# A tuned transformer kernel: the norm's root mean square applied to a product's output, and weight loads issued one stage earlier

## The reference

```python
def rmsnorm(x, g):
    y = x * lax.rsqrt(jnp.mean(x * x, axis=-1, keepdims=True) + EPS)
    return y * g

def swiglu(h, w_in, w_out):                       # w_in 1024 x 5632, w_out 2816 x 1024
    gate, up = jnp.split(h @ w_in, 2, axis=-1)
    return (jax.nn.silu(gate) * up) @ w_out

for i in range(2):                                # first block
    x = x + 0.5 * swiglu(rmsnorm(x, ffn_norm[i, 0]), ffn_w_in[i, 0], ffn_w_out[i, 0])
    h = rmsnorm(x, mix_norm[i])
    x = x + (chunked_sgu, pool_mixer)[i](h, ...)  # both begin with h @ w_in
    x = x + 0.5 * swiglu(rmsnorm(x, ffn_norm[i, 1]), ffn_w_in[i, 1], ffn_w_out[i, 1])
x = rmsnorm(x, final_norm)
```

## Time and profile before

| | us |
|---|---|
| median of 3 runs (3184.03 to 3192.28) | 3188.72 |
| the profiled execution | 3189.99 |
| its span | 3188.0 |
| PE busy in the span | 2776.1 (87%) |
| DVE busy | 1315.2 (41%) |
| ACT busy | 887.9 (28%) |
| mean granted clock of PE | 0.934 |

### The profile page before, as it was taken

One profiled execution on the slowest core, in us unless ns is written; L12 is line 12 of the kernel. 1 busy time (PEld: TensorE's weight loads), 2 busy tenths in 40 slices (PEclk: granted clock), 3 DMA queues, 4 the chain that ended last, 5 costly groups with the idle time before them and its releaser, 6 DMA issues. The chain is left out here.

```text
span 3188.0 us, 44602 instructions
## 1 busy us (share of the span) xinstructions
PE 2776.1 (87%) x18276; PEld 2130.9 (67%) x18276; DVE 1315.2 (41%) x1781; ACT 887.9 (28%) x960; POOL 8.6 (0%) x13
## 2 busy tenths in 40 slices
PE   7989889899889967566999999999999699776888
PEld 6989889899779936354444444444444388666887
DVE  4534445455355412543324322222122338134893
ACT  4424334254234311231111112122112162122441
POOL 0000000000000000000000000000000000000000
PEclk9999899999989978686999999999999899988999
DMA  5635346345245571107999999999999533320551
GB/s 178 234 109 159 119 145 236 109 159 183 95 155 184 218 271 80 53 1 276 417 415 416 416 415 416 416 417 418 417 417 418 209 106 119 133 105 13 173 197 66
DMA packets 278879, 724.10 MB, mean 227 GB/s; under 512 B 18913, under 2 KB 177197, under 8 KB 243789
## 3 DMA queue, kind: packets, MB, share of 16 engines
q1 hardware_dynamic: 278434, 722.34, 59.7%
q10 hardware_dynamic: 330, 0.10, 0.0%
HBM read 721.35 MB, written 1.05 MB: 227 GB/s over the span
## 5 line engine op out<-in xcount | busy, mean ns | idle before, releaser
L505 PE MATMUL bank<-h_high,weight_parts 128*128 128x256 f32 x4352 | 785.3, 283 | 7.4 <-DVE weight_parts L493 7.4
L505 PEld LDWEIGHTS bank<-h_high,weight_parts 128*128 128x128 f32 x4352 | 672.9, 189 | 9.3 <-issue 9.0
L493 DVE TENSOR_TENSOR weight_parts<-weight_slots,weight_parts 128x2048 fp32r<-128x2048 f32 x208 | 472.7, 2289 | 342.6 <-ACT weight_parts L487 342.6
L487 ACT ACTIVATE weight_parts<-weight_slots 128x2048 fp32r<-128x2048 f32 x208 | 394.7, 1911 | 546.3 <-DMA weight_slots<-in_ffn_w_in 192.4
L2119 PE MATMUL bank<-weight_slots,item_x 128*64 128x512 f32 x2176 | 476.1, 595 | 0.7 <-ACT item_x L2192 0.7
L505 PE MATMUL bank<-h_part,weight_parts 128*128 128x256 f32 x1680 | 476.1, 283 | 0.0
L2119 PEld LDWEIGHTS bank<-weight_slots,item_x 128*64 128x64 f32 x2176 | 153.7, 137 | 298.8 <-issue 298.0
L2275 DVE TENSOR_TENSOR expert_sum_then_keys<-bank,expert_sum_then_keys 128x512 f32<-128x512 f32 x136 | 84.5, 684 | 625.8 <-PE bank L2158 625.8
L505 PE MATMUL bank<-hidden_high,weight_parts 128*128 (+1 forms) x1760 | 314.0, 280 | 3.8 <-DVE weight_parts L493 3.8
L505 PEld LDWEIGHTS bank<-h_part,weight_parts 128*128 128x128 f32 x1680 | 317.1, 189 | 0.1
L505 PEld LDWEIGHTS bank<-hidden_high,weight_parts 128*128 128x128 f32 x1760 | 270.8, 189 | 4.2 <-issue 4.2
(11 more groups left out here) (446 smaller groups left out, 2707.3 us busy)
## 6 DMA issues: line engine op xcount, KB each, us to landing
weight_slots<-in_w_mlp SPq DMA_DIRECT2D x408, 1024.0 KB, 21.1
weight_slots<-in_ffn_w_in SPq DMA_DIRECT2D x88, 1024.0 KB, 5.2
weight_slots<-in_ffn_w_out SPq DMA_DIRECT2D x44, 1024.0 KB, 7.2
weight_slots<-in_w_ada SPq DMA_DIRECT2D x24, 1024.0 KB, 13.0
weight_slots<-in_ffn_w_up SPq DMA_DIRECT2D x22, 1024.0 KB, 5.2
weight_slots<-in_a_w_in SPq DMA_DIRECT2D x16, 1024.0 KB, 6.3
weight_slots<-in_w_in SPq DMA_DIRECT2D x16, 1024.0 KB, 5.6
weight_slots<-in_ffn_w_down SPq DMA_DIRECT2D x11, 1024.0 KB, 7.3
```

The source lines that it names most:

```text
L487: K.nc.scalar.activation(high, source, ACT.Copy).then_inc(K.high_written.sem, 1)
L493: K.nc.vector.tensor_tensor(low, place, high.bitcast(F32), ALU.subtract)\
L505: m = K.nc.tensor.matmul(out, stationary[a], moving[b], start=start and n == 0, stop=stop and n == 2, **flags)
```

## The change

Nine norms lose their block. In a new class `LateNorm`, which works within the stage, DVE writes the operand x * g at once (8 tensor_scalar), PE starts the first unit on it as its tiles come, and the squares are summed beside it: ACT squares, DVE adds the four chunks into one (3 instructions), PE runs 2 products against ones between the halves of the first unit (in `dense_down` behind the unit). In the two stages with outputs by token it also runs 4 products with one moving column. Root and reciprocal follow the operand's splits. Every output of the stage is then multiplied by rstd as it leaves its bank: by DVE, one 128x512 tensor_tensor a bank (`scaled`), or by the scale of an ACT instruction, two 128x256 in place of one 128x512 (`token_gelu`, `token_values`). In `SiluGate` and `ConvGate` DVE scales both banks of a pair into SBUF, and silu and taps read from there. In `spatial_gate` the gelus read SBUF. In `two_branches` DVE scales `K.h` itself once at the end of `dense_up`, since later products read it.

The ten `rmsnorm` that remain sum the squares by the same 3 additions and 2 products (the two over fewer tiles keep theirs).

The first 6 units (8 in `spatial_gate`, 4 in `pool_mixer`) of these nine stages are issued by SP in the stage ahead: in `setup` behind the rows; in the products down behind their last load; in the norm block ahead for `two_branches` (gate2, line 2000) and for the convolution (xa_post, line 3026). The loads of `cross_attention`'s product were already issued ahead.

```diff
-            for t in range(tiles):
-                if t % per == 0:
-                    pe.wait_ge(*K.squares(t // per + 1))
-                last = nc.tensor.matmul(K.ps[7][:, 0:S], K.ones, squares[:, t, :], start=t == 0, stop=t == tiles - 1)
+            pe.wait_ge(*(K.squares_added(1) if chunks > 1 else K.squares(1)))
+            for t in range(per):
+                last = nc.tensor.matmul(K.ps[7][:, 0:S], K.ones, squares[:, t, :], start=t == 0, stop=t == per - 1)
             last.then_inc(K.banks.full[7], 1)
...
+            for c in range(1, chunks):
+                dve.wait_ge(*K.squares(c + 1))
+                added = nc.vector.tensor_tensor(squares[:, 0:per, :], squares[:, 0:per, :],
+                                                squares[:, c * per:(c + 1) * per, :], ALU.add)
+                if c < chunks - 1:
+                    K.vsteps.link(added)
+                else:
+                    added.then_inc(K.squares_added.sem, 1)
...
+class LateNorm:
...
+    def __init__(self, K, gain, bank=0, rows=False):
+        self.K, self.gain, self.rows, self.at = K, gain, rows, K.banks.take(bank)
+        self.width = S + TB * rows
...
+    def write_operand(self, dve):
+        K, v = self.K, self.K.nc.vector
+        for t in range(DT):
+            m = v.tensor_scalar(K.h[:, t, :], K.x[:, t, :], self.gain(t), None, ALU.mult)
+            if t % 2:
+                m.then_inc(K.operand.sem, 1)
+    def add_squares(self, dve, squares):
+        K, v = self.K, self.K.nc.vector
+        for c in range(1, 4):
+            dve.wait_ge(*K.squares(c + 1))
+            added = v.tensor_tensor(squares[:, 0:2, :], squares[:, 0:2, :], squares[:, 2 * c:2 * c + 2, :], ALU.add)
+            if c < 3:
+                K.vsteps.link(added)
+        added.then_inc(K.squares_added.sem, 1)
+    def await_operand(self, eng, tiles=DT):
+        eng.wait_ge(*self.K.operand((tiles + 1) // 2))
+    def sum_squares(self, pe, squares):
+        K, b = self.K, self.at[0]
+        K.banks.vacant(pe, self.at)
+        pe.wait_ge(*K.squares_added(1))
+        for t in range(2):
+            m = K.nc.tensor.matmul(K.ps[b][:, 0:S], K.ones, squares[:, t, :], start=t == 0, stop=t == 1)
+        for block in range(TB if self.rows else 0):
+            for t in range(2):
+                m = K.nc.tensor.matmul(K.ps[b][:, S + block:S + block + 1], squares[:, t, block * P:(block + 1) * P],
+                                       K.ones[:, 0:1], start=t == 0, stop=t == 1)
+        m.then_inc(K.banks.full[b], 1)
+    def root(self, act):
+        K, b = self.K, self.at[0]
+        K.banks.ready(act, self.at)
+        K.nc.scalar.activation(K.rstd[:, 0:self.width], K.ps[b][:, 0:self.width], ACT.Sqrt, bias=K.col("eps"), scale=1.0 / D)\
+            .then_inc(K.banks.free[b], 1)
+    def invert(self, dve):
+        K = self.K
+        K.banks.read(dve, self.at)
+        K.nc.vector.reciprocal(K.rstd[:, 0:self.width], K.rstd[:, 0:self.width]).then_inc(K.rstd_written.sem, 1)
+        dve.wait_ge(*K.rstd_written(1))
...
+def scaled(K, out, ps):
+    return K.nc.vector.tensor_tensor(out, ps[:, :].rearrange("p (t s) -> p t s", t=2),
+                                     K.rstd[:, 0:S].unsqueeze(1).broadcast_to([P, 2, S]), ALU.mult)
...
                 if u == 1:
+                    if norm is not None:
+                        norm.await_operand(act)
                     write_high(K, high, src[:, 2:, :])
+                    if norm is not None:
+                        norm.root(act)
...
+            K.vsteps.eng = dve
+            if norm is not None:
+                norm.write_operand(dve)
+                norm.add_squares(dve, squares)
...
                     leave_low(K, dve, K.high_written(2), src[:, 2:, :], high, low[:, :, :])
+                    if norm is not None:
+                        norm.invert(dve)
...
+                    norm.await_operand(act)
                     write_high(K, flat(K.h_high[:, :, :]), flat(src[:, :, :]))
+                    norm.root(act)
+                if j == ahead:
+                    act.wait_ge(*K.rstd_written(1))
...
+                    norm.invert(dve)
+            K.vsteps.eng = dve
+            norm.write_operand(dve)
+            norm.add_squares(dve, squares)
...
+def first_unit(K, pe, slot, ps, norm, squares):
+    for half in range(2):
+        for k in range(DT):
+            if half == 0 and k % 2 == 0:
+                norm.await_operand(pe, k + 2)
+            last = K.nc.tensor.matmul(ps[:, half * 256:(half + 1) * 256], slot[:, k * 256 + half * P:k * 256 + (half + 1) * P],
+                                      K.h[:, k, :], start=k == 0, stop=k == DT - 1)
+        if half == 0:
+            norm.sum_squares(pe, squares)
+    return last
...
+class PairWeights:
+    def __init__(self, K, w_in):
+        self.ring, self.view, self.issued = K.ring, w_in.rearrange("(t p) n -> p t n", p=P), False
+        trips = (FF // 256 - 1) // 2
+        self.units = [[K.ring.take(n) for _ in range(2)] for n in (1, trips, trips)]
+    def issue(self, sp):
+        if self.issued:
+            return
+        self.issued = True
+        for pair, units in enumerate(self.units):
+            for g, unit in enumerate(units):
+                self.ring.vacant(sp, unit)
+                self.load(sp, unit, pair * 256 + g * FF)
...
+            norm.square(act, squares)
             split(0, first_up[0][1], 3)
+            norm.await_operand(act)
             write_high(K, flat(K.h_high[:, :, :]), flat(K.h[:, :, :]))
+            norm.root(act)
...
+            norm.write_operand(dve)
+            norm.add_squares(dve, squares)
             split(0, 0, 1, first_up[0][1], 3)
             leave_low(K, dve, K.high_written(2), flat(K.h[:, :, :]), flat(K.h_high[:, :, :]), flat(h_low[:, :, :]))
+            norm.invert(dve)
...
-        K.nc.vector.tensor_tensor(hid[:, bass.ds(pair * 2, 2), :], self.silu[:, b, :].rearrange("p (t s) -> p t s", t=2),
-                                  K.ps[up][:, :].rearrange("p (t s) -> p t s", t=2), ALU.mult)\
-            .then_inc(banks.free[up], 1)
...
+        K.nc.scalar.activation(part, part, ACT.Silu).then_inc(K.gelus.sem, 1)
+    def dve(self, dve, i, pair, b, at, hid, high, low):
+        K, banks, ((gate, _, gate_full), (up, _, up_full)) = self.K, self.K.banks, at
+        dve.wait_ge(banks.full[gate], i + (gate_full + 1))
+        scaled(K, self.buf[:, b, 0:2, :], K.ps[gate]).then_inc(banks.free[gate], 1)
+        dve.wait_ge(banks.full[up], i + (up_full + 1))
+        scaled(K, self.buf[:, b, 2:4, :], K.ps[up]).then_inc(banks.free[up], 1)
+        dve.wait_ge(banks.free[up], i + (at[1][1] + 2))
+        dve.wait_ge(K.gelus.sem, pair + (K.gelus.base + 1))
+        K.vsteps.link(K.nc.vector.tensor_tensor(hid[:, bass.ds(pair * 2, 2), :], self.buf[:, b, 0:2, :], self.buf[:, b, 2:4, :],
+                                                ALU.mult))
+        split_hidden(K, pair, hid, high, low)
...
+        act.wait_ge(K.taps.sem, i * 2 + (K.taps.base + b + 1))
...
+        scaled(K, self.scaled[:, 0:2, :], K.ps[gate]).then_inc(banks.free[gate], 1)
         dve.wait_ge(banks.full[up], i + (up_full + 1))
+        scaled(K, self.scaled[:, 2:4, :], K.ps[up]).then_inc(banks.free[up], 1)
+        dve.wait_ge(banks.free[up], i + (at[1][1] + 2))
...
+            first.issue(sp)
...
+        def token_gelu(j):
+            def write(ps):
+                for b in range(TB):
+                    m = nc.scalar.activation(v[:, b, j * 256:(j + 1) * 256], ps[:, b * 256:(b + 1) * 256], ACT.Gelu_apprx_tanh,
+                                             scale=K.rstd[:, S + b:S + b + 1])
+                return m
+            return write
...
+        def column_gelu(which, eng, j, out):
+            if which == "act" and 0 <= j - 3 < 8:
+                banks.read(eng, out[j - 3])
+                part = u[:, 2 * (j - 3):2 * (j - 3) + 2, :]
+                nc.scalar.activation(part, part, ACT.Gelu_apprx_tanh)
...
+            jobs.append((None, False, "dve", lambda ps, j=j: scaled(K, u[:, 2 * j:2 * j + 2, :], ps)))
...
+        dense_down(K, K.h, w_in, store_scaled_to(K, p), norm=LateNorm(K, lambda t: K.param("mix_norm", DT + t), bank=7))
...
+        rmsnorm(K, M.sum[:, :, :], None, lambda t: K.gate2[:, t:t + 1], DT, add_to=K.x[:, :, :], loads=following.issue)
...
+                if j == len(jobs):
+                    nc.vector.tensor_tensor(K.h[:, :, :], K.h[:, :, :], K.rstd[:, 0:S].unsqueeze(1).broadcast_to([P, DT, S]), ALU.mult)
...
-        rmsnorm(K, K.x[:, :, :], K.h, lambda t: K.param("norm_xa_pre", t), DT)
         w_o = DownWeights(K, a["xa_wo_3"][0], DT)
-        dense_down(K, K.h, w_q, store_to(K, q), w_o)
+        dense_down(K, K.h, w_q, store_scaled_to(K, q), w_o, LateNorm(K, lambda t: K.param("norm_xa_pre", t), bank=7))
+        following = later()
...
+    ahead.append(PairWeights(K, w_in[0, 0]))
+    setup(K, a, const, ahead[-1])
```

(61 more changed lines are left out.)

196 lines of the change are left out of this document (114 added, 82 removed).

## The result

The changed kernel takes **3100.0 us** in the median of 4 runs (3096.46 to 3103.26), the kernel before 3188.5 (3184.03 to 3192.28): 88.5 us less, a ratio of 0.9719 with a 95% interval of 0.9705 to 0.9733. The forecast was 3094.0, in a range of 3074 to 3122.

The account below looks back on a forecast made before the run. PE bounds the swiglu loops, DVE the convolution's, and waits lie between stages; 100.5 + 8.3 - 6.1 - 7.6 - 0.3 = 94.8 us off 3190.0 gives 3095, median 3094. Own range 3082 to 3108, with rivals 3074 to 3122.

Parts of the forecast that it names:

- The nine stretches: From a norm's first square to the first product by parts, nine times: 201.6 us become 101.1, 100.5 less.
- the low parts: DVE's two low parts of the operand in a late-norm stage: end at 9.0 us, ahead of PE at 10.3.
- the rival that priced them: Loads still start with the stage, so the second unit is 4 us later in eight stages: 3126; chance 0.06.
- the second unit by parts: Rival: the norm's waits return here, such as by a late low part, 3 us in nine stages: 3121; chance 0.05.
- DVE's new work in the swiglus: Two scalings a pair in the swiglu loops, about 1.5 us, covered by PE; without that cover 66 us.
- The norm ahead of the two branches: gate2's norm: six issues of 12.98 us in a block of 13.4, covered by 0.4, about 1 us at stake.
- The column products: 4 one-column products added in each of two stages: 1.2 us taken, bounds 0.9 and 3.3.
- the fall of the clock: In the nine stages' first products, the same fall as line 316 shows in the kernel before: 17.7 us.
- The convolution: Loop over pairs, scaling on DVE without cover: net 0.69 us a pair, 7.6 lost for 11.
- Setup: Six issues added to setup's block, which ends at 24.0 and not 18.2: 6.1 us lost with the block's change.
- The other norms: Eight 8-tile norms keeping their block: 5.1 us each to the sums, 9.6 gained, of which 8.3 kept.
- spatial_gate: At the stage's end two ACT instructions stand for one: 0.3 us lost.

Follow-up runs that it names:

- the filling: Five products of constants ending PE's work in the five blocks ahead of late-norm stages, against the kernel with two setup loads and convolution operand scaled once: 3080.7 us against 3087.5.
- setup_two: Changed kernel, but setup issues two of the first stage's six loads and the stage itself the other four: 3093.3 us, 6.8 less than the changed kernel.
- the first experiment: Changed kernel, but the eight sets of weights issued a stage ahead are issued at the start of the stage that uses them: 3132.0 us.

## Why the prediction was right, and where it was off

**The mechanism held, step by step.** The nine stretches came to 96.4 us for 101.1. The order of the engines at the third boundary is the one forecast: the additions end 4.27 us after the first square (4.4), the low parts 8.7 (9.0), PE decides. PE idles once in each stage, as said; the 3.6 us hold in five of the nine, in the others it is 8.6 or 9.0 (the third block's were 9.0 before the change too). Loads late gave 3132.0; the rival that priced them said 3126. No wait came back at the second unit by parts, and DVE's new work in the swiglus is covered, 1.6 us a pair for 1.5. The norm ahead of the two branches takes 13.71 us from its first square to the next; 13.4 was worked out, so its six issues hid as said.

**The stretches were over-priced by 4.7 us.** At full clock a stretch takes 8.73 with the filling, where 0.7 + 8.3 = 9.0 had been put, nine times 0.27; in the two stages of `dense_down` it takes 0.28 less again. The 8.3 scaled the 3.69 of the earlier trace rows by 18/8, and so counted the length of its last record more than once: 36 records in a row take 7.94. The column products cost 0.8 a stage and not 1.2. With the filling's numbers the nine would be five of 8.73 (the swiglus and the convolution), two of 8.45 (`dense_down`) and two of 9.53 (those with column products), 79.6 us together. That is an estimate: only five of the nine ran with the filling. By it the fall of the clock cost 96.4 - 79.6 = 16.8. The forecast took 17.7 for it from the earlier trace rows, so the 4.7 are 2.4 + 0.6 + 0.8 + 0.9: that the clock would fall as it did before was right, and the last experiment shows that it can be had back.

**The convolution was under-priced by 4.0 us: the term furthest off.** "Its 4 first taps, 1.90 from PSUM, should take 1.14 from SBUF" was priced by the tensor_scalar of the earlier trace rows. It took 1.38 for four, 0.41 each where that one takes 0.35. That one has one column of scalars as an operand and does one operation, this one has two of each; whether this is the reason was not tested. The two scalings took 1.28, as forecast, and the wait behind them 0.28 where 0.15 had been put. So a pair pays 1.28 + 0.28 - 0.52 + 0.04 = 1.08 for 0.69, and eleven pairs 11.9; 11.6 is what the traces show. That the other taps would gain nothing was right: 1.67 from SBUF, 1.65 from PSUM. The Trainium skill, VectorE: DVE Perf Modes, section on the TRN2 errata, gives an overhead by which an operation from SBUF saves 65 ns; with it on the 8 other taps the prediction's estimate of the loss was 2 us. This case's rows don't show a flat 65: nothing is saved per scalar_tensor_tensor, 130 ns per tensor_scalar.

**Setup, 1.5 more.** The block was to end at 24.0, from 12.55 and 11.46 for six issues. They began at 12.77 and took 12.68. The rule used, that a block ends with its last issue, is what `setup_two` confirmed.

**The other norms, 2.1 less.** The term was 5.1 us to the end of the sums; it is 5.52 everywhere. The additions end at 3.33, as forecast, and the products start at 3.47, but take 2.04 and not 1.65: a quarter of the 6.61 counts only a quarter of what stands once in every group, the longer first distance (0.55) and the last record's whole length (0.63), the opposite of the slip in the stretches. Eight times 0.4 is 3.4 us; 1.3 of it was kept in reserve.

**`spatial_gate`, 1.1 more.** The part behind its stretch took 162.2 to 162.9 us in the three traces with the norm in a block, and 163.9 to 164.7 in the nine with the late norm. So the loss is real. Of the 1.4 some 0.8 lie in the stage's product down, whose 336 records start 120.5 ns apart for 118.3 before; see the first point of the last section.

**The rest is scatter in the main.** Stretches with the same code in every kernel scatter between traces: the mixed attention with its norm took 221.9 to 227.4 us over twelve traces, the experts with theirs 1082.0 to 1087.1. Where the account has +1.6 for everything else, it holds, without the norms' sums, +5.2 from the first, -2.5 from the second, +2.3 from the two branches and -4.2 from the four swiglus (last section). A single pair of profiles can't tell less than some 5 us apart outside the loops.

**That the sum came within 6 us is in part luck.** The stretches gave 4.7 us more than forecast, and the other terms together 10.3 less; the two kinds of error had different causes and happened to have opposite signs.

## What to carry to other kernels

What an edit is worth can depend on another edit: the early loads cost 7 us alone and gave 32 once the work they feed could start at once, while the late norm gave 56 of the 88 us without them. So price a part of a change in the kernel that holds the other part. Moving a scale from an operand to its outputs is free in a loop that the matmul engine bounds and costs its full price, in every turn, in one that the vector engine bounds; there it pays to take the chain once, ahead of the loop. Count an issue that is moved on the block that it moves into: the block ends with the last issue, even if nobody needs the data yet. And price a group of records by the distance of their starts plus one last record; scaling a group's whole time by its count was wrong here in both directions.

## What had not been expected of the hardware

- The same by-parts products run at one of two paces, at a granted clock of 1.00 in both. In the first loop of a swiglu of the code before, the mean distance of two records is 117.8 ns in some stages and 120.0 in others; from the first product by parts to the next norm's first square five of its twelve swiglus in three traces take 184.07 us and seven 186.30. The second loop, the product down, had 117.8 in all twelve. In the nine traces with the late norm the first loop had 117.8 and the second 120.0 in all 36 swiglus, 185.25 together. So the -1.05 us a swiglu in the pair of profiles is made of two parts: 2.2 gained in the first loop, which is chance of the profiled execution before, whose four were all of the slower kind there, and 1.2 lost in the second, which comes with the change every time. What sets the pace stays open.
- Six issues in a row of 1 MB each, 256 columns of a wider matrix in rows of 1 KB, held SP for 11.1 to 14.5 us in every trace (48 such groups), with nothing else under way too (13.14 in the first experiment's row). The first takes 0.4 to 0.5 us there, each of the last three 2.8 to 4.5. The bytes alone don't decide it: in the trace of before six issues of 1 MB in rows of 4 KB (two of `w_branch_ssm`, four of `w_out`, from 2762.20) held SP for 3.85 us, and a single one of either kind holds it for 0.37. What does decide it was not tested.
- Between unbroken products ahead of it and the first unit behind it an idle time of 1.44 us left the clock at its upper level, one of 3.60 us did not. The length of the gap alone doesn't tell: with two loads in setup PE idled only 1.82 us ahead of the first unit, and its first 16 records took 6.74 us, at a granted clock of 0.50. There PE had done little before the gap: 1.09 us of products, behind 4.10 of idling.
